# Fourteen more projection slabs as high and low parts, the low parts made by GpSimd

## The reference

```
h = rmsnorm(x, norm_mix)
proj = h @ w_in                                   # 2048 x 7168
conv_in = proj[..., :2048]                        # glu and sigmoid halves
ssm_in  = proj[..., 2048:3072]
gate_in = proj[..., 3072:]
branch_conv = conformer_conv(conv_in, ...)        # 31-tap depthwise convolution, layer norm, silu
branch_ssm  = s5_ssm(ssm_in, ...)                 # grouped state-space scan over the 256 tokens
gates  = sigmoid(gate_in + b_gate)
merged = gates[0] * branch_conv + gates[1] * branch_ssm
x = x + merged @ w_out
```

## Time and profile before

| what | value |
|---|---|
| median of 3 runs | 2510.77 us (2508.38 to 2511.92) |
| the profiled execution, its time | 2506.04 us |
| the profiled execution, its span | 2504.0 us |
| PE busy over the span | 2151.4 us (86%) |
| DVE, ACT, POOL busy | 64%, 24%, 27% |
| mean granted clock of PE | 0.99 of full speed |

### The profile page before, as it was taken

One profiled execution on the slowest core, in us unless ns is written; L12 is line 12 of the kernel. 1 busy time (PEld: TensorE's weight loads), 2 busy tenths in 40 slices (PEclk: granted clock), 3 DMA queues, 4 the chain that ended last, 5 costly groups with the idle time before them and its releaser, 6 DMA issues. The chain is left out here.

```text
span 2504.0 us, 24427 instructions
## 1 busy us (share of the span) xinstructions
PE 2151.4 (86%) x9666; PEld 1474.6 (59%) x9666; DVE 1611.0 (64%) x2404; ACT 608.5 (24%) x964; POOL 669.4 (27%) x524
## 2 busy tenths in 40 slices
PE   9999999999999999999967777777776877777776
PEld 8888887889889989888832222222222322222232
DVE  7766677688989885564995656574445444444444
ACT  4345555432143524442110000000101000000000
POOL 0000000000000000001456545555443645444541
PEclk9999999999999999999989999999999999999999
DMA  6544444534445444555989999999999999999997
GB/s 230 187 168 169 168 168 152 202 135 152 161 142 185 154 166 152 187 192 208 415 351 421 421 421 422 422 421 422 422 422 422 422 422 422 422 421 422 421 422 315
DMA packets 103504, 747.96 MB, mean 299 GB/s; under 512 B 11617, under 2 KB 11617, under 8 KB 12897
## 3 DMA queue, kind: packets, MB, share of 16 engines
q0 software_dynamic: 73728, 536.90, 51.6%
q1 hardware_dynamic: 29376, 209.20, 23.2%
q10 hardware_dynamic: 288, 0.31, 0.0%
HBM read 744.28 MB, written 2.10 MB: 298 GB/s over the span
## 5 line engine op out<-in xcount | busy, mean ns | idle before, releaser
L746 PE MATMUL ps<-slots 128*128 128x512 f32 x736 | 342.3, 609 | 116.6 <-DMA slots<-in_peer_v,slots 116.6
L1128 DVE TENSOR_TENSOR weight_low<-weight_raw,weight_high 128x2048 fp32r<-128x2048 f32 x146 | 334.1, 2289 | 119.7 <-ACT weight_high L760 119.6
L505 PE MATMUL ps<-operand_parts,weight_high 128*128 128x512 f32 x1504 | 369.7, 398 | 8.0 <-DVE operand_parts L1380 3.9
L746 PE MATMUL ps<-weight_raw,slots 128*128 128x512 f32 x608 | 282.5, 609 | 103.2 <-DMA weight_raw<-in_peer_v,slots 103.2
L1620 DVE SCALAR_TENSOR_TENSOR slots<-slots,work 128x2048 f32<-128x2048 f32 x100 | 228.6, 2291 | 204.7 <-DMA slots<-in_peer_u,slots 204.5
L746 PEld LDWEIGHTS ps<-slots 128*128 128x128 f32 x736 | 134.4, 192 | 323.7 <-issue 239.4
L505 PEld LDWEIGHTS ps<-operand_parts,weight_high 128*128 128x128 f32 x1504 | 278.7, 189 | 69.8 <-issue 5.0
L760 ACT ACTIVATE weight_high<-weight_raw 128x2048 fp32r<-128x2048 f32 x146 | 278.6, 1908 | 97.1 <-PE ps L508 94.4
L423 POOL IOTA slots<- 128x16 f32 x1 | 0.1, 144 | 1041.7 <-DVE slots L1506 1041.7
L1079 ACT ACTIVATE slots<-ident,slots 128x128 f32<-128x128 f32 x242 | 85.7, 395 | 790.9 <-PE ps L746 515.8
L746 PEld LDWEIGHTS ps<-weight_raw,slots 128*128 128x128 f32 x608 | 111.2, 192 | 274.2 <-issue 203.5
(11 more groups left out here) (230 smaller groups left out, 2638.9 us busy)
## 6 DMA issues: line engine op xcount, KB each, us to landing
weight_raw<-in_w_in SPq DMA_DIRECT2D x120, 1024.0 KB, 4.8
weight_raw<-in_w_out SPq DMA_DIRECT2D x32, 1024.0 KB, 4.8
weight_raw<-in_peer_w_q SPq DMA_DIRECT2D x16, 1024.0 KB, 9.0
weight_raw<-in_conv_w_out SPq DMA_DIRECT2D x8, 1024.0 KB, 4.8
weight_raw<-in_ssm_w_val SPq DMA_DIRECT2D x8, 1024.0 KB, 4.8
weight_raw<-in_ssm_w_gate SPq DMA_DIRECT2D x8, 1024.0 KB, 4.8
residual_t<-in_x SPq DMA_DIRECT2D x4, 512.0 KB, 6.0
out_y<-work SPq DMA_DIRECT2D x4, 512.0 KB, 5.4
```

The lines of the kernel that those rows point to most:

```text
L505: nc.tensor.matmul(out, high[:, k, :], o_parts[:, :, place(k), :], start=(k == order[0]), stop=False)
L746: mm = nc.tensor.matmul(ps_v[:, c, :], diag[:, n % 16, :], rows[b][:, c * 512:(c + 1) * 512], start=False, stop=False, skip_group_check=True)
L1128: v.tensor_tensor(w_low[:, s % NSLAB, :], w_raw[:, s % NSLAB, :], w_high[:, i % NHIGH, :], ALU.subtract).then_inc(w_low_ready, 1)
```

## The change

The last 14 tiles of the branch stage, t = 10 to 23, are computed split instead of plain (SPLIT_GATE moves up by 14, the lists of split slabs and tiles grow). ACT makes their high parts. Their low parts are made by POOL, which gets 14 `tensor_tensor` subtractions of 128 x 2048, in place, each behind `w_high_ready`, and counts them in a semaphore of its own, `pool_low_ready`. PE waits for that semaphore in these 14 tiles; `vector_lows` turns a slab's number into DVE's count elsewhere. DVE's queue is not edited.

```diff
--- before.py
+++ after.py
@@ -92,13 +92,21 @@
 PLAIN = 2
 SPLIT_OUT = 64 - PLAIN
 SPLIT_BRANCH = SPLIT_OUT + 16
-SPLIT_GATE = SPLIT_BRANCH + 4
+SPLIT_GATE = SPLIT_BRANCH + 18
 SPLIT_VG = SPLIT_GATE + 32
 SPLIT_OUT2 = SPLIT_VG + 16
 SPLIT_AT = 6
-SPLIT_SLABS = [*range(PLAIN, 80), *range(80 + SPLIT_AT, 80 + SPLIT_AT + 4), *range(80 + 24, 80 + 56), *range(80 + 56 + 8, 80 + 56 + 8 + 32)]
-SPLIT_TILES = [*range(TILE_IN + PLAIN, TILE_IN2), *range(TILE_IN2 + SPLIT_AT, TILE_IN2 + SPLIT_AT + 4), *range(TILE_GATE, TILE_CV),
+POOL_LOW = SPLIT_BRANCH + 4
+SPLIT_SLABS = [*range(PLAIN, 80), *range(80 + SPLIT_AT, 80 + 24), *range(80 + 24, 80 + 56), *range(80 + 56 + 8, 80 + 56 + 8 + 32)]
+SPLIT_TILES = [*range(TILE_IN + PLAIN, TILE_IN2), *range(TILE_IN2 + SPLIT_AT, TILE_GATE), *range(TILE_GATE, TILE_CV),
                *range(TILE_VG + 1, TILE_OUT2, 2), *range(TILE_OUT2, TILE_WQ)]
+
+
+
+def vector_lows(i):
+
+    return i + 1 if i < POOL_LOW else i + 1 - (SPLIT_GATE - POOL_LOW)
+
 
 O_OUT, O_GATE, O_Z, O_OUT2 = KD, 2 * KD, 3 * KD, 3 * KD + KH
 
@@ -293,7 +301,7 @@
         eps_ready = sem("eps_ready")
         x_paired, x_squared = sem("x_paired"), sem("x_squared")
         proj_done, proj_freed = sem("proj_done"), sem("proj_freed")
-        w_high_ready, w_low_ready = sem("w_high_ready"), sem("w_low_ready")
+        w_high_ready, w_low_ready, pool_low_ready = sem("w_high_ready"), sem("w_low_ready"), sem("pool_low_ready")
         o_high_ready, o_low_ready = sem("o_high_ready"), sem("o_low_ready")
         misc_done, misc_freed = sem("misc_done"), sem("misc_freed")
         bu_done, bu_freed, cy_done, skip_ready = sem("bu_done"), sem("bu_freed"), sem("cy_done"), sem("skip_ready")
@@ -419,6 +427,11 @@
                                         fill=-3.0e38, base=0, pattern=[[-1, P]],
                                         channel_multiplier=1).then_inc(mask_ready, 1)
 
+            for i in range(POOL_LOW, SPLIT_GATE):
+                at = split_slab(i) % NSLAB
+                pool.wait_ge(w_high_ready, i + 1)
+                nc.gpsimd.tensor_tensor(w_low[:, at, :], w_raw[:, at, :], w_high[:, i % NHIGH, :], ALU.subtract).then_inc(pool_low_ready, 1)
+
             pool.wait_ge(merged, KD)
             nc.gpsimd.iota(iota16, pattern=[[1, 16]], base=0, channel_multiplier=0,
                            allow_small_or_imprecise_dtypes=True).then_inc(zero_ready, 1)
@@ -484,7 +497,10 @@
                         pe.wait_ge(o_low_ready, ready(k))
                     nc.tensor.matmul(out, high[:, k, :], o_high[:, place(k), :], start=(k == order[0]), stop=False)
                     nc.tensor.matmul(out, high[:, k, :], o_low[:, place(k), :], start=False, stop=False)
-                pe.wait_ge(w_low_ready, i + 1)
+                if POOL_LOW <= i < SPLIT_GATE:
+                    pe.wait_ge(pool_low_ready, i - POOL_LOW + 1)
+                else:
+                    pe.wait_ge(w_low_ready, vector_lows(i))
                 for k in order:
                     mm = nc.tensor.matmul(out, low[:, k, :], o_high[:, place(k), :], start=False, stop=(k == order[-1]))
                 mm.then_inc(proj_done, 1)
@@ -648,7 +664,7 @@
             pe.wait_ge(misc_freed, M_B + 4)
             first = BRANCH.index(("ssm", 0)) + 1
             for t in range(len(BRANCH)):
-                if SPLIT_AT <= t < SPLIT_AT + 4:
+                if t >= SPLIT_AT:
                     split_product(SPLIT_BRANCH + t - SPLIT_AT, ready=(lambda k: O_GATE + k + 1) if t == SPLIT_AT else None)
                 else:
                     tile(TILE_IN2, t, normed_in, ready=(lambda k: (h_scaled, KD + k + 1)) if t == 0 else None)
@@ -950,7 +966,7 @@
                 read_out(TILE_IN2, t, slot(BRANCH_SLOT[kind] + n), ACT.Sigmoid if kind == "sig" else ACT.Copy)
                 if t in (SPLIT_AT - 3, SPLIT_AT - 2):
                     split_high(SPLIT_BRANCH + t - SPLIT_AT + 3)
-                elif t in (SPLIT_AT, SPLIT_AT + 1):
+                elif SPLIT_AT <= t < len(BRANCH) - 2:
                     split_high(SPLIT_BRANCH + t - SPLIT_AT + 2)
                 if first <= t < first + 4:
                     ssm_inputs(t - first)
```

## The result

The changed kernel takes 2567.38 us (median of 4 runs, 2565.62 to 2568.29), the kernel before 2509.61 on the same terms: a ratio of 1.0234, 95% interval 1.0222 to 1.0246. That is 57.8 us slower. The profiled execution took 2568.29 us, 62.25 more than that of before.

The account below looks back on a forecast made before the run. PE sets the pace, with DVE nearly as full. POOL holding DVE (+59.4 us) and the slowed clock (+2.7) give +62.1 on 2506.0, 2568.1, and with 4.7 added about 2573 us; range 2520 to 2593.

Parts of the forecast that it names:

- Exclusion: Beside scan(0), each POOL subtraction reading SBUF blocks DVE's two-SBUF-input operations for its whole length; chance 0.72.
- a tile on PE, split against plain: Branch-stage tiles 10 to 23 on PE: 5.76 us each split instead of 6.91 plain, saving 1.15 us a tile.
- start of the scan, after the ACT copy: DVE's scan(0) starts about 1.0 us later, at 580.2 us, because ACT's first new copy delays the copies feeding it.
- one subtraction on POOL: Each of POOL's 14 two-input subtractions of 128 x 2048 takes 4.6 us, bounds 1.8 and 9.3.
- DVE time lost to POOL: During scan(0), DVE loses 2.6 us to the first subtraction and 59.8 to the other 13, 62.4 in all.
- low part 0 done: DVE finishes the low part of gate slab 0 at 742.8 us, against 679.4 before.
- PE's wait for it: In gate tile 0, PE arrives at 667.3 us and stands for 75 us until DVE's low part is ready.
- clock after the wait: PE's granted clock is 0.50 for the first 5.33 us of work after its idle, losing 2.7 us.
- The room in DVE's queue: Gate slab 0's low part stands behind scan(0) on DVE, so PE can win only 3.9 us even with POOL free.
- POOL paying alone: Rival: POOL waits for DVE, which loses nothing; each subtraction takes 9.2 us, +29.5 us, total 2540 us; chance 0.09.
- No exclusion: Rival: POOL's subtractions do not hold DVE during the scan; -0.2 us, total 2510.6 us; chance 0.12.
- Clearly faster: Rival: gate slab 0's low part would come more than 5 us before 678, though no DVE work is removed; chance 0.03.

## Why the prediction was right

**Exclusion**, the step that decided the sign, held, and in the direction that no row of before had: POOL's subtraction holds DVE for its length. It rested on two gather issues that ended 0.80 and 0.81 us after a DVE operation and a third that took 0.94 with DVE idle, and on the Trainium skill's rule (SBUF — State Buffer, Who interferes with whom), for which no row of before had a waiting DVE. The whole trace of before bears the gathers out: 240 of its 512 gather issues start inside a DVE operation of this form, and their ends lie 0.80 to 0.82 us behind its end (10 to 90%). The experiments now show it for this kernel: it needs a read by POOL (a write alone doesn't do it) and, on DVE, SBUF inputs in one of the two forms tried, two inputs or the 0.42 us form with one; with one input from SBUF and the other from PSUM it is absent.

**The terms**, with the 1.45 us taken off by which this execution was late already at the branch stage's first tile (521.87 against 520.40):

| term | predicted | measured |
|---|---|---|
| a tile on PE, split against plain | 1.15 us | 96.69 / 14 - 80.64 / 14 = 1.15 |
| start of the scan, after the ACT copy | 580.2 | 581.62 - 1.45 = 580.17 |
| one subtraction on POOL | 4.6 us | 4.62, at most 5.09 |
| DVE time lost to POOL | 62.4 us | 148.4 - 88.9 = 59.5 |
| low part 0 done | 742.8 | 741.30 - 1.45 = 739.85 |
| PE's wait for it | 75 us | 72.44 |
| clock after the wait | 2.7 us | (3.79 - 2.08) + (6.34 - 5.76) = 2.3 |
| a new wait for low part 1 | none | none |

The largest miss is the time lost on DVE, 2.9 us too much: the sum took all of POOL's 4.6 us for each, but an operation is held for 4.37 us (5.06 - 0.69), 0.25 less than POOL's operation lasts. The price on POOL, an addition of a memset and twice the reading share of a select, came out to within 0.02 us, and that was luck: the same addition gives 3.2 us for a copy, which took 1.89.

**The whole** agrees better than its parts, by luck: the sum said 62.1 us more, and the two profiled executions are 62.25 apart. Gate tile 1 is read at 751.51 against 691.23, 60.28 later; of these 1.45 are the early lateness, so 58.8 are the change's (predicted: 59.4 + 2.7 = 62.1). The remaining 1.9 of the 62.2 us between the two spans lie behind the gate stage. The medians, 57.8 apart, are nearer to the 58.8. The 4.7 us that I added to get from the profiled execution to a median were too much for the changed kernel, whose profiled execution was slower than its median by 0.9; part of them may be the early lateness, which the profiled execution of before, unlike most of the others, did not have.

**The room in DVE's queue.** "Even a free POOL lets PE win only these 3.9 us" was right: without POOL's work the kernel measured 0.9997 of before. So exclusion made the change slow, but its absence would not have made it fast: low part 0 stood behind a scan that ended no sooner. No run pairs a POOL that holds nothing with a reordered DVE queue, so what fourteen tiles could give there is open.

**The rivals.** POOL paying alone would have shown waits of L505 for POOL; there is none. No exclusion gave 0.2 us less than before by my sum; the kernels in which it is really absent came out 1.2 below before (POOL's small and large memsets; both intervals hold 1) and, in one run, 1.1 above. Under "Clearly faster" the 5 us are counted twice: the bound is 5 us before 683.35, which is the 678 named there.

## What to carry to other kernels

Before moving work to an idle engine, ask what it shares with the busy one. Here each microsecond of an operation with which POOL read SBUF was taken nearly in full from a DVE that worked on two operands in SBUF, so half the price would have been to let DVE do it. Where DVE took one of its operands from PSUM, POOL's 14 subtractions cost it nothing. And find first who sets the end of the stretch: the place in the queue of one low part, not the count of matmuls, decided what 16 us saved on PE were worth. A few tiles with the queue reordered around DVE's real waits gave 0.12%; fourteen gave nothing in the old order of the queue, even with their low parts for free.

## What the runs showed that I had not expected

- POOL's copy of 128 x 2048 float32 takes 1.89 us against 1.81 for a memset: one read costs it almost nothing beside its write, while the subtraction with two reads takes 4.62. My addition, with 0.69 ns a column for each read, gave the right sum for two inputs and gives 3.2 for one.
- PE's granted clock fell to 0.50 for 3.4 us early in this execution, and not in that of before. Windows of PE from 155.9 us in the changed kernel and in the kernel before:

```profile
155.90:159.30 3.40, 3.13 (x6) 0.50 0.45 186
```

```profile
155.90:159.30 3.40, 3.03 (x12) 1.00 0.41 169
```

  The code there is the same in both. It accounts for the 1.45 us (the next low-part matmuls start at 162.29 instead of 160.87), and differences of this size between single executions should not be read as an edit's. The profiled execution of before is the exception here: in 9 of the 11 experiments, the one with four more tiles among them, the granted clock in this window is between 0.50 and 0.76, and only in two is it 1.00.
- After 280 dummy products and then 9.94 us of idle the low-part matmuls ran in 3.78 us, as slowly as after 72.44 us of idle (3.79) or 13.07 (3.78). The length of these waits made no difference.
